# FFN loop: four of eight k-pairs of gate and up as 2x2 block products with seven multiplications

## The chip, the cores and the metric

The kernel runs on one core of one Trainium2 chip. The metric is the time of the core on the device, in microseconds (us); each kernel is run several times and the median counts. Beside the times there is one profiled execution, which gives the time of every instruction on TensorE (PE; its weight load is PEld), VectorE (DVE), ScalarE (ACT), GpSimd (POOL) and in SyncE's queue (SP).

## What is computed

One block of a streaming encoder: retention heads and a state-space group side by side, then a dense SwiGLU FFN. SEQ is 256, D_MODEL 2048, D_FF 5632, all in float32. The change touches the FFN alone:

```python
h = rmsnorm(x, norm_ffn_g[l])
x = x + (jax.nn.silu(h @ w_gate[l]) * (h @ w_up[l])) @ w_down[l]
```

## The kernel before

Every product is made of three matmuls on parts. A float32 matrix is split into a high part (rounded to the matmul's format) and a low part (what is left), and x·w is taken as hi·hi + lo·hi + hi·lo. So each weight is loaded from HBM into `raw`, rounded by ScalarE into `w_hi` (`high`, L492), and VectorE subtracts to get `w_lo` (`low`, L837). `raw`, `w_hi` and `w_lo` have four slots each (RAW = SPL = 4).

The unit of work is a chunk: two k-blocks of 128 rows by 512 columns (512 KB). `column_chunk` (L1510 on, its matmuls L1517) multiplies a chunk with the 256 tokens: 3 parts x 2 k-blocks x 2 halves of 128 tokens = 12 matmuls of 128x128 by 512 columns. The tokens' blocks are the stationary operand, `h2` of `actA` for k-blocks 0 to 7 and of `h2B` for 8 to 15.

D_FF is worked off in 11 groups (FG) of 512 columns. The first group's gate and up chunks, 16 of them (FFN0 to LOOP0), come ahead of the loop. A turn of the loop then has 24 chunks (TURN): 8 of gate and 8 of up of the next group, one k-pair each, and 8 of down of the group before (4 columns of 512, 2 chunks each). There are ten turns, nine in a hardware loop and one written out, and then the tail: 8 down chunks of the last group, and the final norm.

What sets the order: each engine has its program in order, and semaphores count. ScalarE's `high` waits for the data of its chunk (d_raw) and until TensorE has done the chunk four back (pe_done); VectorE's `low` waits for high_done; TensorE's `ready` waits for low_done; SyncE's `load` of the chunk four ahead waits for low_done too. Gate's sum stands in PSUM banks 0 and 1, up's in 2 and 3, down's columns alternate between banks 6, 7 and 4, 5. ScalarE takes silu of gate as soon as gate's 8 chunks are done (`silu`, L767), VectorE multiplies it with up (`ff`, L1152), transposes in blocks (`turn_blocks`, L1179), and SyncE moves the blocks to their places (`move`, L377: two moves behind each of the loads of chunks 5 to 12 of the next turn, the first pair waiting for the transposes). From these ScalarE and VectorE make `ffT_hi` (L772) and `ffT_lo` (L1185) for the down chunks. VectorE adds each down column into x (`down_col`, L1195); TensorE waits for that add (cols_added) before it uses the banks again, two columns later.

## Time and profile before

| | us |
|---|---|
| median of 3 runs | 1118.73 |
| lowest, highest | 1118.14, 1119.39 |
| span of the profiled execution | 1116.8 |
| TensorE busy | 1104.5 |
| VectorE busy | 731.2 |
| ScalarE busy | 533.2 |

The span is what the profiler saw from the first to the last instruction of one execution. Busy time of TensorE is made of matmuls that overlap: a row's own length (389 ns in the list by lines) is longer than the step from one to the next. A row with a count x4 stands for four in a row, with the time from the first's start to the last's end. A step from one operation to the next is read from two starts.

### The profile page before, as it was taken

The numbers are of one execution on the slowest core, as the hardware profiler recorded it, in microseconds if no ns is written. First come the engines' busy times: TensorE is split into PE (matmuls) and PEld (weight loads), VectorE is DVE, ScalarE is ACT, GpSimd is POOL, SyncE is SP. The second block draws the span as 40 slices with busy tenths as digits, with TensorE's granted clock in tenths as the row PEclk, the third lists the DMA queues.
The fourth block names the chain that finished last, engine by engine and source line by source line (L and its number), as shares of the span: only waits on it lengthen the run. The fifth ranks groups of instructions, "written<-read, shape, count | busy, mean of one in ns | idle before, by whom it ended". The sixth has DMA issues, their size and how long they took to land.

```text
span 1116.8 us, 15234 instructions
## 1 busy us (share of the span) xinstructions
PE 1104.5 (99%) x5506; PEld 914.2 (82%) x5506; DVE 731.2 (65%) x811; ACT 533.2 (48%) x640; POOL 106.9 (10%) x162
## 2 busy tenths in 40 slices
PE   9999999999999999999999999999999999999997
PEld 7878778888988888888888888888888888888886
DVE  7999998655865754564655646465564656556477
ACT  7569444345743663434434343443434344443443
POOL 7130233320100500000000000000000000000010
PEclk9999999999999999999999999999999999999999
DMA  9884688854665775867676766757676675757663
GB/s 361 283 227 136 191 225 262 256 167 150 234 207 196 211 225 187 253 196 212 189 212 197 202 198 192 217 189 209 198 204 197 193 214 193 208 194 204 203 209 111
DMA packets 131478, 232.15 MB, mean 208 GB/s; under 512 B 12016, under 2 KB 29808, under 8 KB 130800
## 3 DMA queue, kind: packets, MB, share of 16 engines
q1 hardware_dynamic: 126192, 220.35, 64.0%
q0 software_dynamic: 4832, 10.36, 3.7%
q10 hardware_dynamic: 416, 0.92, 0.2%
q8 instruction: 25, 0.41, 0.1%
q14 instruction: 13, 0.11, 0.0%
HBM read 218.09 MB, written 5.11 MB: 200 GB/s over the span
## 4 chain that ended last, share of the span: by engine, by line
PE 84%; DVE 10%; DMA 3%; issue 2%; ACT 1%; POOL 0%; SPq 0%; POOLq 0%; DVEq 0%; ACTq 0%
PE ps L1517 71%; DVE w_lo L837 4%; PE ps L1542 3%; PE ps L1535 3%; PE ps L1539 3%; DMA raw<-in_w_in 2%; DVE wb L964 1%; DVE wb L962 1%; DVE wb_t L963 1%; PE ps L1817 1%; PE ps L1818 1%; PE ps L1819 1%; PE ps L1650 0%; DVE cl_t L1037 0%; DMA swapped<-state 0%
## 5 line engine op out<-in xcount | busy, mean ns | idle before, releaser
L837 DVE TENSOR_TENSOR w_lo<-raw,w_hi 128x1024 fp32r<-128x1024 f32 x384 | 467.9, 1224 | 355.5 <-ACT w_hi L492 354.6
L492 ACT ACTIVATE w_hi<-raw 128x1024 fp32r<-128x1024 f32 x383 | 406.1, 1061 | 551.5 <-PE ps L1517 428.3
L1517 PE MATMUL ps<-w_hi,actA_hi 128*128 128x512 f32 x416 | 111.4, 390 | 0.0
L1517 PE MATMUL ps<-w_hi,actA_lo 128*128 128x512 f32 x416 | 111.2, 389 | 0.0
L1517 PE MATMUL ps<-w_lo,actA_hi 128*128 128x512 f32 x416 | 111.2, 389 | 0.0
L1517 PE MATMUL ps<-w_hi,h2B_hi 128*128 128x512 f32 x352 | 94.1, 389 | 0.0
L1517 PE MATMUL ps<-w_hi,h2B_lo 128*128 128x512 f32 x352 | 94.1, 389 | 0.0
L1517 PE MATMUL ps<-w_lo,h2B_hi 128*128 128x512 f32 x352 | 94.1, 389 | 0.0
L1517 PEld LDWEIGHTS ps<-w_hi,actA_lo 128*128 128x128 f32 x416 | 78.1, 188 | 16.2
L1517 PEld LDWEIGHTS ps<-w_lo,actA_hi 128*128 128x128 f32 x416 | 78.1, 188 | 16.2
L1517 PEld LDWEIGHTS ps<-w_hi,actA_hi 128*128 128x128 f32 x416 | 77.9, 188 | 16.0
L1517 PE MATMUL ps<-w_hi,ffT_hi 128*128 128x512 f32 x320 | 85.5, 389 | 0.0
L1517 PE MATMUL ps<-w_hi,ffT_lo 128*128 128x512 f32 x320 | 85.5, 389 | 0.0
L1517 PE MATMUL ps<-w_lo,ffT_hi 128*128 128x512 f32 x320 | 85.5, 389 | 0.0
L377 POOL DMA_DIRECT2D ff_moved<-ff_turned x24 | 12.9, 543 | 706.9 <-DVE ff_turned L1179 706.9
L1517 PEld LDWEIGHTS ps<-w_hi,h2B_lo 128*128 128x128 f32 x352 | 66.1, 188 | 13.7
L1517 PEld LDWEIGHTS ps<-w_hi,h2B_hi 128*128 128x128 f32 x352 | 66.1, 188 | 13.7
L1517 PEld LDWEIGHTS ps<-w_lo,h2B_hi 128*128 128x128 f32 x352 | 66.1, 188 | 13.7
L1517 PEld LDWEIGHTS ps<-w_hi,ffT_hi 128*128 128x128 f32 x320 | 60.1, 188 | 12.5
L1517 PEld LDWEIGHTS ps<-w_hi,ffT_lo 128*128 128x128 f32 x320 | 60.1, 188 | 12.5
L1517 PEld LDWEIGHTS ps<-w_lo,ffT_hi 128*128 128x128 f32 x320 | 60.1, 188 | 12.4
L1195 DVE TENSOR_TENSOR x<-ps,x 128x1024 f32<-128x1024 f32 x40 | 48.7, 1218 | 0.0
(279 smaller groups left out, 1261.4 us busy)
## 6 DMA issues: line engine op xcount, KB each, us to landing
raw<-in_w_gate SPq DMA_DIRECT2D x88, 512.0 KB, 4.6
raw<-in_w_up SPq DMA_DIRECT2D x88, 512.0 KB, 4.7
raw<-in_w_down SPq DMA_DIRECT2D x88, 512.0 KB, 4.3
raw<-in_w_in SPq DMA_DIRECT2D x79, 512.0 KB, 5.3
raw<-in_w_out SPq DMA_DIRECT2D x32, 512.0 KB, 4.2
...
raw<-in_ssm_w_glu SPq DMA_DIRECT2D x8, 512.0 KB, 3.4
```

The source lines that it names most:

```text
L377: eng.dma_start(moved[32 * b:32 * b + 32, :, a].rearrange("p t k j -> p t (k j)"), turned[32 * a:32 * a + 32, b].rearrange("p t k j -> p t ...
L492: nc.scalar.activation(w_hi[:, s % SPL], raw[:, s % RAW], ACT.Copy).then_inc(S["high_done"], 1)
L837: tt(w_lo[:, s % SPL], raw[:, s % RAW], w_hi[:, s % SPL].bitcast(F32), ALU.subtract).then_inc(S["low_done"], 1)
L962: tt(o, of_groups(b_re, b, LOC - 1), of_powers(pr, b, 1, LOC - 1), ALU.mult)
L963: link(tt(t, of_groups(b_im, b, LOC - 1), of_powers(pi, b, 1, LOC - 1), ALU.mult))
L964: tt(o, o, t, ALU.add).then_inc(S["wb_ready"], 1)
L1195: tt(cols, ps[:, b0:b0 + 2], cols, ALU.add).then_inc(S["cols_added"], 1)
L1517: ins = mm(ps[:, banks + t], blocks[k][kind == 1][:, tok], w[:, s, at], start=first and kind == 0 and k == 0, stop=last and kind == 2 and ...
L1535: mm(ps[:, banks + t], blocks[k][0][:, tok], w_hi[:, s, at], start=first and k == 0, stop=False)
L1539: mm(ps[:, banks + t], blocks[k][1][:, tok], w_hi[:, s, at], start=False, stop=False)
L1542: ins = mm(ps[:, banks + t], blocks[k][0][:, tok], w_lo[:, s, at], start=False, stop=last and k == 1)
L1817: mm(o, w_hi[:, n % SPL, at], hi, start=first, stop=False)
```

## The change

Gate and up of the same k-pair are now taken together as one pair of chunks, gate's k-pair u in chunk 2u and up's in chunk 2u+1; SyncE loads them in that order. A pair is a product of 2x2 blocks: the tokens' blocks A (2 halves of tokens x 2 k-blocks), the weights' blocks B (2 k-blocks x gate, up). UNITS = "CSCSSCSC" names the pairs 0 to 7: in C (plain) the product takes 8 block products, in S (mixed) 7, by Strassen's scheme in Winograd's form. Each block product is three matmuls, so a plain pair issues 24 and a mixed pair 21.

A mixed pair needs four sums of token blocks (made once, ahead of the loop: `h_column`, `combos`, `combo_high`, `combo_low`), and of weight blocks for every pair anew: VectorE makes four blocks `mix` from raw (`mix_sums`, three operations, two of which wait for the one before), ScalarE rounds them (`mix_high`, 2048 columns), VectorE takes the low part (`mix_low`, 2048 columns). Of the second chunk of the pair only the second half needs a high and a low part of its own (`high_second`, `low_second`, 512 columns). `mix` is one buffer, `mix_hi` and `mix_lo` have two.

The plain pairs add into the same banks as the mixed ones, so they too give sums that are put together at the end: four banks (0 to 3) take plain and mixed products, three (4 to 6) the mixed ones' alone. `first_product`, `first_sums` and `last_sums` put gate and up together in `mix`; silu and `ff` now read `mix`. Banks 4 to 6 are also down's, so pair 1 waits for column 3's add of the turn before and for ff, and down's first column for `first_sums`. VectorE's add of column 3 moves behind the mixed sums of the next turn's pair 1. In `mixed_unit`, TensorE does three products (9 matmuls) on the plain weights, gives both slots back, waits for `mix_low`, and does four (12). g_final shares its place with `mix_lo`; its load moves from ahead of the loop into the tail, behind the last moves.

The core of the diff:

```diff
+UNITS = "CSCSSCSC"
+MIXED = tuple(u for u in range(GRP) if UNITS[u] == "S")
+PLAIN = tuple(u for u in range(GRP) if UNITS[u] == "C")
+NM = len(MIXED)
+B_P2, B_P3, B_P4, B_P5, B_P1, B_P6, B_P7 = range(7)
+COMBO_AT = tuple(FFN0 + 6 + 3 * c for c in range(4))
...
-                        w = A["w_gate"] if c < GRP else A["w_up"]
-                        k = 2 * (c % GRP)
+                        w = A["w_gate"] if c % 2 == 0 else A["w_up"]
+                        k = 2 * (c // 2)
...
+                    sp.wait_ge(S["mix_free"], 1 + NM * (FG - 1))
+                    sp.dma_start(g_final[:], A["g_final"]).then_inc(d_gfin, 16)
...
+            def mix_high(c, turn=None):
+                q = mixed_at(c)
+                act.wait_ge(S["mix_step"], count(turn, 3 * NM, 3 * q + 3))
+                if turn is not None:
+                    act.wait_ge(S["mix_free"], count(turn, NM, q))
+                nc.scalar.activation(mix_hi[:, q % 2], mix[:], ACT.Copy).then_inc(S["mix_high"], 1)
...
+            def mix_sums(c, turn=None):
+                q = mixed_at(c)
+                for s in (LOOP0 + c, LOOP0 + c + 1):
+                    dve.wait_ge(d_raw[s % RAW], count(turn, 16 * TURN // RAW, 16 * (s // RAW + 1)))
+                if c % TURN // 2 != MIXED[0]:
+                    dve.wait_ge(S["mix_low"], count(turn, NM, q))
+                elif turn is not None:
+                    dve.wait_ge(S["ff_ready"], turn + 2)
...
+            def last_sums(j):
+                dve.wait_ge(S["pe_done"], j * TURN + (LOOP0 + 2 * GRP))
+                dve.wait_ge(S["sum_step"], j * 4 + 2)
+                tt(mix[:, 1::2], mix[:, 1:3], ps[:, B_P5].unsqueeze(1).to_broadcast([P, 2, NCOL]), ALU.add
+                   ).then_inc(S["sum_step"], 1)
+                dve.wait_ge(S["sum_step"], j * 4 + 3)
+                tt(mix[:, 0:3], ps[:, B_P2:B_P4 + 1], mix[:, 0:3], ALU.add).then_inc(S["sum_step"], 1)
...
+            def mixed_unit(u, s, q, turn, fresh, done):
+                (a11, a12), (_, a22) = tokens(u, 0), tokens(u, 1)
+                s1, s2, s3, s4 = ([s_mixed[part][MIXED.index(u)][:, k] for part in range(2)] for k in range(4))
+                ends = products([(B_P2, a12, 1), (B_P1, a11, 0), (B_P3, s4, 3)], w_blocks(w_hi, s), w_blocks(w_lo, s),
+                                fresh, done)
+                ends[B_P1].then_inc(S["pe_done"], 1)
+                ends[B_P3].then_inc(S["pe_done"], 1)
+                pe.wait_ge(S["mix_low"], count(turn, NM, q + 1))
+                hi, lo = ([x[:, q % 2, b] for b in range(4)] for x in (mix_hi, mix_lo))
+                ends = products([(B_P5, s1, 0), (B_P6, s2, 2), (B_P7, s3, 1), (B_P4, a22, 3)], hi, lo, fresh, done)
+                ends[B_P4].then_inc(S["mix_free"], 1)
...
+                    if u == MIXED[0]:
                         pe.wait_ge(S["ff_ready"], j + 1)
+                        pe.wait_ge(S["cols_added"], j * 4 + 8)
...
                     if c == 2 * GRP:
                         pe.wait_ge(S["ffT_lo_ready"], j + 1)
+                        pe.wait_ge(S["sum_step"], j * 4 + 2)
```

How it stands in the programs, taken from the last turn of the loop, the one that is written out. TensorE before, gate of k-pairs 1 and 2 (a wait in brackets is a semaphore by name):

```order
L1517 MATMUL ps<-w_hi,actA_hi 128x512 [waits low_done]
L1517 MATMUL ps<-w_hi,actA_hi 128x512 x3
L1517 MATMUL ps<-w_hi,actA_lo 128x512 x4
L1517 MATMUL ps<-w_lo,actA_hi 128x512 x4
L1517 MATMUL ps<-w_hi,actA_hi 128x512 [waits low_done]
L1517 MATMUL ps<-w_hi,actA_hi 128x512 x3
L1517 MATMUL ps<-w_hi,actA_lo 128x512 x4
L1517 MATMUL ps<-w_lo,actA_hi 128x512 x4
```

TensorE after, pair 1, a mixed one, up to the last of its mixed blocks:

```order
L1782 MATMUL ps<-w_hi,actA_hi 128x512 [waits low_done,cols_added,ff_ready]
L1782 MATMUL ps<-w_hi,actA_hi 128x512
L1782 MATMUL ps<-w_hi,sA_hi 128x512
L1782 MATMUL ps<-w_hi,actA_lo 128x512 x2
L1782 MATMUL ps<-w_hi,sA_lo 128x512
L1782 MATMUL ps<-w_lo,actA_hi 128x512 x2
L1782 MATMUL ps<-w_lo,sA_hi 128x512
L1782 MATMUL ps<-mix_hi,sA_hi 128x512 [waits mix_low]
L1782 MATMUL ps<-mix_hi,sA_hi 128x512 x2
L1782 MATMUL ps<-mix_hi,actA_hi 128x512
L1782 MATMUL ps<-mix_hi,sA_lo 128x512 x3
L1782 MATMUL ps<-mix_hi,actA_lo 128x512
```

Between the ninth and the tenth matmul of the pair there is now a wait for `mix_low`, and the wait for low_done at its head counts both chunks. VectorE before, from chunk 4 of the last turn to the product with silu (13 chunks in the first row):

```order
L837 TENSOR_TENSOR w_lo<-raw,w_hi 128x1024 [waits high_done] x13
L1185 TENSOR_TENSOR ffT_lo<-ff_moved,ffT_hi 128x8x4x32 [waits ffT_hi_ready]
L837 TENSOR_TENSOR w_lo<-raw,w_hi 128x1024 [waits high_done] x3
L1152 SCALAR_TENSOR_TENSOR ff_act<-ps,rstd,ff_act 128x512 [waits silu_ready,pe_done]
L1152 SCALAR_TENSOR_TENSOR ff_act<-ps,rstd,ff_act 128x512
```

VectorE after, pairs 3 and 4, both mixed:

```order
L1311 TENSOR_TENSOR mix<-raw 128x1024 [waits mix_low,d_raw3,d_raw2]
L1314 TENSOR_TENSOR mix<-raw,mix 128x512 [waits mix_step]
L1316 TENSOR_TENSOR mix<-raw,mix 128x512 [waits mix_step]
L939 TENSOR_TENSOR w_lo<-raw,w_hi 128x1024 [waits high_done]
L1297 TENSOR_TENSOR w_lo<-raw,w_hi 128x512 [waits high_done]
L1322 TENSOR_TENSOR mix_lo<-mix,mix_hi 128x2048 [waits mix_high]
L1311 TENSOR_TENSOR mix<-raw 128x1024 [waits mix_low,d_raw1,d_raw0]
L1314 TENSOR_TENSOR mix<-raw,mix 128x512 [waits mix_step]
L1316 TENSOR_TENSOR mix<-raw,mix 128x512 [waits mix_step]
L939 TENSOR_TENSOR w_lo<-raw,w_hi 128x1024 [waits high_done]
L1297 TENSOR_TENSOR w_lo<-raw,w_hi 128x512 [waits high_done]
L1322 TENSOR_TENSOR mix_lo<-mix,mix_hi 128x2048 [waits mix_high]
```

Where one low half stood for each chunk, a mixed pair has three sums, a whole and a half low part and a mixed low part, and pair 4's sums stand behind pair 3's mixed low part. VectorE before, around the end of up and the first down column:

```order
L1185 TENSOR_TENSOR ffT_lo<-ff_moved,ffT_hi 128x8x4x32 [waits ffT_hi_ready]
L837 TENSOR_TENSOR w_lo<-raw,w_hi 128x1024 [waits high_done] x3
L1152 SCALAR_TENSOR_TENSOR ff_act<-ps,rstd,ff_act 128x512 [waits silu_ready,pe_done]
L1152 SCALAR_TENSOR_TENSOR ff_act<-ps,rstd,ff_act 128x512
L837 TENSOR_TENSOR w_lo<-raw,w_hi 128x1024 [waits high_done]
L1179 STREAM_TRANSPOSE ff_turned<-ff_act 128x4x4x32 [waits d_moved,ff_ready]
L1179 STREAM_TRANSPOSE ff_turned<-ff_act 128x4x4x32
L837 TENSOR_TENSOR w_lo<-raw,w_hi 128x1024 [waits high_done]
L1195 TENSOR_TENSOR x<-ps,x 128x2x512 [waits cols_added,pe_done]
```

VectorE after, the same place:

```order
L939 TENSOR_TENSOR w_lo<-raw,w_hi 128x1024 [waits high_done]
L1334 TENSOR_TENSOR mix<-ps,mix 128x512 [waits p1_ready]
L1336 TENSOR_TENSOR mix<-ps,mix 128x512 [waits sum_step]
L1342 TENSOR_TENSOR mix<-mix,ps 128x2x512 [waits sum_step,pe_done]
L1345 TENSOR_TENSOR mix<-ps,mix 128x1536 [waits sum_step]
L939 TENSOR_TENSOR w_lo<-raw,w_hi 128x1024 [waits high_done] x2
L1261 SCALAR_TENSOR_TENSOR ff_act<-mix,rstd,ff_act 128x512 [waits silu_ready]
L1261 SCALAR_TENSOR_TENSOR ff_act<-mix,rstd,ff_act 128x512
L939 TENSOR_TENSOR w_lo<-raw,w_hi 128x1024 [waits high_done]
L1371 STREAM_TRANSPOSE ff_turned<-ff_act 128x4x4x32 [waits d_moved,ff_ready]
L1371 STREAM_TRANSPOSE ff_turned<-ff_act 128x4x4x32
L939 TENSOR_TENSOR w_lo<-raw,w_hi 128x1024 [waits high_done]
```

The four sums, the third of which waits for TensorE's last pair, now stand ahead of the low halves of chunks 18 and 19.

## Rows read from the trace of the kernel before

**Rows 1.** Page, part 1; then the chain from 400 us on.

```profile
PE 1104.5 (99%) x5506; PEld 914.2 (82%) x5506; DVE 731.2 (65%) x811; ACT 533.2 (48%) x640; POOL 106.9 (10%) x162
by line: PE ps L1517 97.5%; PE ps L1508 0.5%; PE ps L1507 0.5%; PE ps L1506 0.5%; DVE x_gain L1338 0.1%; POOLq L165 0.1%; ACT y1T L805 0.1%; DVE x L1323 0.1%; DVEq L165 0.1%; POOL ss L1496 0.0%; issue 0.0%; DVEq L1337 0.0%; POOLq L1494 0.0%
```

**Rows 2.** Windows: length, busy us of PE, PEld, DVE, ACT, POOL, granted clock, DMA.

```profile
500.04:565.32 65.28, 65.28 (x290) 54.07 (x288) 37.63 (x33) 27.57 (x27) 0.00 (x0) 1.00 0.68 201
1110.00:1116.80 6.80, 0.00 (x0) 0.00 (x0) 2.50 (x7) 1.44 (x3) 0.92 (x2) 0.81 0.65 250
```

**Rows 3.** Timeline, one chunk: start, us, engine, operation, count, [idle before, releaser].

```profile
714.92 1.07 PE L1517 MATMUL ps<-w_hi,h2B_hi 128*128 128x512 f32 x4
715.12 1.06 ACT L492 ACTIVATE w_hi<-raw 128x1024 fp32r<-128x1024 f32 x1 [1.66 <-PE ps L1517]
...
716.21 1.23 DVE L837 TENSOR_TENSOR w_lo<-raw,w_hi 128x1024 fp32r<-128x1024 f32 x1 [1.49 <-ACT w_hi L492]
...
717.64 1.07 PE L1517 MATMUL ps<-w_hi,actA_hi 128*128 128x512 f32 x4
```

**Rows 4.** By form, TensorE's weight load and VectorE: count, busy us, mean ns.

```profile
L1517 PEld LDWEIGHTS ps<-w_hi,actA_lo 128*128 128x128 f32 x416 | 78.1, 188 | 16.2
L1052 DVE TENSOR_TENSOR qr<-qs,rope 128x512 f32<-128x512 f32 x8 | 5.2, 687 | 5.2 <-PE ps L1641 5.2
```

**Rows 5.** Timeline of VectorE: steps from one operation to the next.

```profile
173.23 1.29 DVE L1052 TENSOR_TENSOR qr<-qs,rope 128x512 f32<-128x512 f32 x2
...
186.53 1.35 DVE L1037 TENSOR_TENSOR cl_t<-c,pi 128x1152 f32<-128x1152 f32 x1
187.92 1.36 DVE L1038 TENSOR_TENSOR cl<-cl,cl_t 128x1152 f32<-128x1152 f32 x1
...
741.83 1.40 DVE L1152 SCALAR_TENSOR_TENSOR ff_act<-ps,rstd,ff_act 128x512 f32<-128x512 f32 x2
...
746.13 1.23 DVE L837 TENSOR_TENSOR w_lo<-raw,w_hi 128x1024 fp32r<-128x1024 f32 x1 [0.28 <-ACT w_hi L492]
747.27 1.22 DVE L1195 TENSOR_TENSOR x<-ps,x 128x1024 f32<-128x1024 f32 x1
```

**Rows 6.** Instructions by form, ScalarE.

```profile
L492 ACT ACTIVATE w_hi<-raw 128x1024 fp32r<-128x1024 f32 x383 | 406.1, 1061 | 551.5 <-PE ps L1517 428.3 <-DMA raw<-in_w_in 56.0 <-PE ps L1542 42.1
L549 ACT ACTIVATE ps<-x_tok 128x2048 f32<-128x2048 f32 x2 | 3.7, 1861 | 0.0
L489 ACT ACTIVATE w_hi<-raw 128x512 fp32r<-128x512 f32 x1 | 0.6, 630 | 0.2 <-DMA raw<-in_w_in 0.2
```

**Rows 7.** DMA issues at 744.8, 761.1, 443.5, 451.2 us; g_final; last: to landing.

```profile
raw<-in_w_gate SPq DMA_DIRECT2D x1, 512.0 KB, 4.5
raw<-in_w_gate SPq DMA_DIRECT2D x1, 512.0 KB, 4.9
raw<-in_w_gate SPq DMA_DIRECT2D x1, 512.0 KB, 5.3
raw<-in_w_up SPq DMA_DIRECT2D x1, 512.0 KB, 6.0
g_final<-in_g_final SPq DMA_DIRECT2D x1, 1024.0 KB, 8.0
```

**Rows 8.** Timelines, the loop's first turn: TensorE's start, SyncE's queue.

```profile
434.76 1.07 PE L1517 MATMUL ps<-w_hi,actA_hi 128*128 128x512 f32 x4
...
440.02 1.27 SPq L377 DMA_DIRECT2D ff_moved<-ff_turned  x2
441.54 0.38 SPq L391 DMA_DIRECT2D raw<-in_w_gate  x1
```

**Rows 9.** Timelines, last down part, tail: TensorE and SyncE's queue.

```profile
1065.80 1.07 PE L1517 MATMUL ps<-w_hi,ffT_hi 128*128 128x512 f32 x4
...
1077.46 13.06 SPq L391 DMA_DIRECT2D raw<-in_w_down  x7
...
1090.28 1.07 PE L1517 MATMUL ps<-w_hi,ffE_hi 128*128 128x512 f32 x4
```

More of the change, by code:

```diff
@@ L328, in h2, with h2_column, count, mixed_at @@
             return (h2B_hi, h2B_lo)[part][:, kb - 8, :]
+        def h2_column(c, part):
+            if c < 2:
+                return (actA_hi, actA_lo)[part][:, 4 * c:4 * c + 4]
+            return (h2B_hi, h2B_lo)[part][:, 4 * c - 8:4 * c - 4]
+        def count(turn, each, n):
+            return n if turn is None else turn * each + n
+        def mixed_at(c):
+            return NM * (c // TURN) + MIXED.index(c % TURN // 2)
+        def mixed_pair(c):
+            return c % TURN < 2 * GRP and c % TURN // 2 in MIXED
+        def column_combos(c):
+            one = 2 * c if 2 * c in MIXED else 2 * c + 1
+            return MIXED.index(one), PLAIN.index(4 * c + 1 - one), one - 2 * c
         def act_block(kb, part):
@@ L690, in side @@
                     x2_square(c)
+                for c in range(4):
+                    if n == COMBO_AT[c] + 2:
+                        combo_high(c)
             def y1T_out(r):
@@ L1145, in out_col_ssm, with ff_first, ff @@
                 last.then_inc(S["cols_added"], 1)
-            def ff(count, chunks):
-                dve.wait_ge(S["pe_done"], chunks)
+            def ff_first():
+                dve.wait_ge(S["pe_done"], LOOP0)
+                dve.wait_ge(S["silu_ready"], 2)
+                for t in range(TOK):
+                    last = stt(ff_act[:, t], ps[:, 4 + t], rstd[:, R_FFN, t:t + 1], ff_act[:, t], ALU.mult, ALU.mult)
+                last.then_inc(S["ff_ready"], 1)
+            def ff(count):
@@ L1277, in _, with down_add @@
                     side(n)
+            for c in range(0, SPL, 2):
+                mixed = mixed_pair(c)
+                if mixed:
+                    mix_sums(c)
+                whole_low(c)
+                side(LOOP0 + c)
+                if mixed:
+                    low_second(c + 1)
+                    mix_low(c)
+                else:
+                    whole_low(c + 1)
+                side(LOOP0 + c + 1)
+            def down_add(j, col):
+                down_col(j * TURN + (LOOP0 + 2 * GRP + 2 * col + 2), j * 4 + (col + 5), col)
             def turn(j, last=False):
                 for c in range(SPL, TURN + SPL):
-                    low(None, turn=j, at=LOOP0 + c)
+                    pair = c < 2 * GRP or c >= TURN and not last
+                    mixed = pair and mixed_pair(c)
+                    if mixed and c % 2 == 0:
+                        mix_sums(c, j)
+                        if c == TURN + 2:
+                            down_add(j, 3)
+                    if mixed and c % 2:
+                        low_second(c, j)
+                        mix_low(c - 1, j)
+                    else:
+                        whole_low(c, j)
                     if c == GRP + SPL + 4:
                         ffT_low(j + 1)
+                    if c == 2 * GRP + 1:
+                        first_sums(j)
+                        last_sums(j)
                     if c == 2 * GRP + 3:
-                        ff(j + 2, j * TURN + (LOOP0 + 2 * GRP))
+                        ff(j + 2)
                     if last and c == 2 * GRP + 4:
@@ L1508, in three, with column_chunk @@
                 return mm(o, x_lo, h, start=False, stop=last)
-            def column_chunk(n, s, blocks, banks, first, last):
+            def column_chunk(n, s, blocks, banks, first, last, frees=None):
                 parts = [(k, t, slice(NCOL * k, NCOL * (k + 1)), slice(P * t, P * (t + 1))) for k in range(2) for t in range(TOK)]
```

213 lines of the change are left out of this document (178 added, 35 removed).

## The prediction

> **What bounds the kernel now.** I read the page first: TensorE is busy 99% of the span and the chain that ended last is almost wholly its matmuls [rows 1]. The windows view then shows that this holds in the loop itself: one turn of the FFN loop takes 65.28 us, TensorE is busy in all of it at a granted clock of 1.00, while VectorE is busy for 38 us and ScalarE for 27.5 us [rows 2]. The timeline of one chunk gives the beat: a chunk of 12 matmuls every 2.72 us, so 0.2267 us each, and 24 chunks in a turn [rows 3]. In the same rows ScalarE rounds a chunk 0.2 us after TensorE has left its slot, VectorE starts its half 1.10 us after that, and both then wait for the next slot. So a turn costs 288 matmuls, and everything else hides. A change that takes matmuls away is worth their beat only as long as the two other engines still hide.
>
> **What goes.** Four of the eight pairs of k-blocks issue 21 matmuls and not 24. That is 12 of 288 in a turn: 12 x 0.2267 = 2.72 us, and 27.2 us over the ten turns. A turn of TensorE alone would be 276 x 0.2267 = 62.56 us. The beat is taken from the row; nothing in it depends on which tile is loaded. The Trainium skill (TensorE: Matmul & The Clock Gate, "Wait — 56ns, not 53.3ns?") has a 512-column matmul at 215.7 ns behind another. The row says 226.7 ns, and the row decides; by the page the gain would be 2.59 us per turn.
>
> **What comes, in engine time.** VectorE's price depends on width only, and neither on SBUF nor PSUM as its source [rows 4, 5]: a 1024-wide operation lets the next one start after 1.14 us; two 512-wide ones together take 1.29 us where one takes 0.687, so a step of 0.60; the rate between them is 1.05 ns per element, which makes 2.22 us for 2048 and 1.68 us for 1536. No row has a tensor_tensor of 2048; the rate is what I have for it. Of width 1152, an operation that waits for the one just before it starts 1.39 us after it, where the rate gives 1.14 + 128 x 1.05 ns = 1.27: 0.11 us more. A mixed pair then takes VectorE 1.25 + 0.71 + 0.60 (the sums, two of them waiting) + 1.14 + 0.60 (the low halves) + 2.22 (the low half of the four mixed blocks) = 6.52 us where it took 2.28. Four of them add 17.0 us. Putting the products together adds 0.71 + 0.60 + 1.25 + 1.68 = 4.2 us. Before, a turn held 24 low halves and 4 column adds (28 x 1.14), the product with silu (1.34), the two transposes (1.27) and the low half of ffT (1.14): 35.7 us. Now it is 56.9 us of 62.6. ScalarE gets 4 x (1.86 + 0.63 - 1.06) + 0.67 = 6.4 us more [rows 6], 34 us in all. So no engine but TensorE is full, but VectorE is at 91%, and in a mixed pair it needs 6.52 us where TensorE needs 21 x 0.2267 = 4.76. What decides is the order within the turn.
>
> **The walk through a steady turn.** T is the time at which TensorE starts pair 0. VectorE gets there with the mixed sums of pair 1, done at T+0.7; column 3's add waited for the last down matmuls and ends at T+1.8; the low halves of chunks 2 and 3 end at T+3.0 and T+3.6. Only then do the slots of raw that pair 3 needs come free. SyncE issues the load of chunk 6 at T+3.1 (0.39 us), then two moves (1.25 us), then chunk 7's at T+4.7. A load lands after 4.5 us when it is alone, after 4.9 with moves beside it, and the second of two in a row after 5.3 [rows 7]. I take 5.3, since this is that case: chunk 7 lands at T+10.0. Before, a slot was refilled in 4.5 us and its chunk came round after 4 x 2.72 = 10.9, so there were 6 us to spare; now the data are wanted at T+8.1, when VectorE is through with pair 2. From there: sums to T+12.6, ScalarE's rounding of 2048 columns to T+14.5, low half to T+16.8. Pair 3 starts at T+15.6 and needs the mixed blocks after 9 matmuls, T+17.7: in time. Pair 4 follows at once as a mixed one: its sums can't start before T+16.8 (one buffer for the sums), end at T+19.3, the low halves of chunks 8 and 9 at T+21.2, its mixed low half at T+23.6. TensorE wants pair 4 at T+20.4 and the mixed blocks 2.0 us later: it waits 0.8, then 0.1, and each wait costs about 0.25 us more, because the weight load (188 ns in [rows 4]) and the start no longer overlap. That is 1.4 us. Pair 6 has the same chain through its loads (issued at T+20.6 and T+22.2, landed T+27.5, mixed low half at T+34.3 against T+34.1): 0.55 us.
>
> The other place is the end of the pairs. VectorE is held at the last sums until pair 7 has ended; call that E. Behind them are queued the low halves of chunks 18 and 19, the product with silu, chunk 20, the transposes, chunk 21 and then the add of column 0, for whose banks column 2 waits: 0.2 + 2.93 + 2.28 + 1.34 + 1.14 + 1.27 + 1.14 + 1.22 = 11.5 us after E, where TensorE comes after 4 chunks, 10.9. With the restart that is 0.9 us. The new wait of column 0 for the first sums costs nothing: pair 7 (5.44 us) hides ScalarE's copy and two 512-wide adds (0.67 + 1.31). Sum: 62.56 + 1.4 + 0.55 + 0.9 = **65.4 us** per turn against 65.28: the 2.72 us go back almost whole.
>
> **Once per run.** In the first turn VectorE arrives late. Before the loop it gets 4 x 3.55 us for the token sums (1.25 + 1.36 + 0.94 each, by widths 1024, 512, 256 and 128), which fill the 1.49 us that it waited per chunk. It reaches the mixed sums of pair 1 only 0.7 us before the loop starts, and then does sums, low halves, the last token sum, mixed low half and the product ff in one piece of 8.8 us; pair 1 waits for ff and is wanted after 5.44: 3.0 us with the restart. The transposes end at 9.4 us after the start of the loop; only then does SyncE issue the moves and behind them the loads of pair 3, as it did before [rows 8]. They land at 17.6 us, the low halves are there at 22.0, pair 3 is wanted at 18.6: 3.7 us. Pair 4 and its mixed blocks follow late by 2.0, pair 6 and column 2 as always, 1.4. So the first turn is 62.56 + 10.1 = 72.7 us. The old first turn had the same late loads, and the four slots hid them. In the tail, the transposes come 2.6 us later and g_final (1 MB, 8.0 us, until now ahead of the loop) lies ahead of the load of chunk 25. That load is issued at 14.8 us after E and not 11.7, lands behind 1 MB more (2 x 1.85 us, two chunks' share by 0.68 of 2.72) at 22.9, and its low half is done at 25.3; TensorE wants it at 24.5 plus the 0.9 from above [rows 7, 9]. I take 0.5 us.
>
> **Sum.** 1116.8 (profiled span) + 9 x 0.1 + 7.4 + 0.5 = 1125.6 us; the waits are sums of small pieces and all on one side, so I round up to 1126.5. The median of the runs is 1.9 us above the span (1118.73): **1128.5 us**, 0.9% slower.
>
> **Bounds.** The turn's waits have unseen parts: the landing of a second load (4.9 to 6.0 in [rows 7], it counts in full in the waits at pair 4 and at pair 6), the restart (0 to 0.25, four times), VectorE's dependent waits (0.11, perhaps 0.05 to 0.2, some eight on the chain). All kind: 1.2 us of waits, 63.8 us per turn, 15 us in all off the forecast. All unkind: 67 us, 16 us on.
>
> **Rivals.** *The matmuls' time is kept.* VectorE has 5.7 us of idle per turn, and if loads land as when alone and restarts are hidden, the walk leaves under 1 us of waits: 63.3 us per turn, 20 us gained, less 7 at the start: 1105 us (1099 to 1113). For it: TensorE never waits now, and half the loads have no move beside them. Against: the chain from T to pair 4 has no slack to begin with. *VectorE's chain becomes the beat.* If the second load takes 6.0 us and each hand-over 0.1 more, pair 4 waits 2.5 us and pair 6 over 1: 66.8 us per turn, 1142 us. It decides from the point where chunk 7 lands later than T+10. *The clock.* The granted clock is 1.00 in all the loop; where TensorE stood idle at the end it is 0.81 [rows 2]. Waits of 3.0 and 3.7 us in the first turn are the longest. If the clock fell to its lower level (1.2 GHz) after one, each 12 matmuls until it rose would cost 2.72 us more, 3 to 5 us once, 1132 us. The Trainium skill has this rule (the same page, "HAM oscillation — how this bites in real kernels"). *That it doesn't do what it says:* the order of instructions has 12 matmuls fewer in each turn, so no.
>
> **Chances.** Forecast (64.9 to 65.9 per turn) 0.42; time kept 0.14; between these two 0.16, of which half ends below 1116.5; VectorE's beat 0.23; clock 0.05. What a measurement can tell from no change is about 0.2%, 2.2 us. So faster 0.22, the same 0.08, slower 0.70. The range leaves out the best case and the worst: 1110 to 1144.
>
> **What would show it.** Right: TensorE's busy share of a middle turn at 96%, turns of 65 to 66 us, its waits at the low halves of pair 4 and at column 2; VectorE about 57 us busy in a turn; first turn near 73 us; loads of chunks 6 and 7 on the path, by a wait of the mixed sums for raw. Wrong: middle turns near 63 us; a 2048-wide operation far from 2.3 us; waits of TensorE at other places; a beat other than 0.2267 us with three or four banks in turn.

## The result, and the profile after

The changed kernel takes **1136.40 us** (median of 4 runs, 1135.68 to 1137.92) against 1118.43 for the kernel before in the same comparison (1117.97 to 1119.39): a ratio of 1.016, 95% interval 1.015 to 1.018. It is slower by 18.0 us, forecast was 9.8. The profiled execution has a span of 1134.4 us against 1116.8.

From the page of the kernel after: busy times (they answer to [rows 1]), and the shares of each engine in the chain that ended last, over the whole span. The third line is the same chain in the kernel before:

```profile
PE 1094.7 (96%) x5386; PEld 891.4 (79%) x5386; DVE 939.1 (83%) x1043; ACT 596.2 (53%) x698; POOL 106.8 (9%) x162
PE 38%; DVE 33%; DMA 11%; issue 8%; ACT 5%; SPq 3%; DVEq 1%; POOL 0%; POOLq 0%; ACTq 0%
PE 84%; DVE 10%; DMA 3%; issue 2%; ACT 1%; POOL 0%; SPq 0%; POOLq 0%; DVEq 0%; ACTq 0%
```

There are 120 matmuls fewer, as intended, and the chain is no longer mostly TensorE: VectorE has a third of it where it had a tenth, and DMA with SyncE's queue 14% where it had 3%. ("issue" is time in which an engine waited for nothing that the profile shows.) The windows view of the kernel after (columns as in [rows 2]) shows the first turn, a middle turn and the tail:

```profile
434.64:507.62 72.98, 66.43 (x277) 53.30 (x276) 60.28 (x60) 33.29 (x32) 0.00 (x0) 0.95 0.60 186
...
573.62:639.58 65.96, 63.79 (x277) 51.49 (x276) 57.16 (x54) 33.49 (x32) 0.00 (x0) 1.00 0.64 199
...
1103.38:1134.40 31.02, 23.84 (x108) 19.85 (x108) 20.79 (x28) 11.93 (x24) 2.61 (x9) 0.89 0.33 121
```

With the starts of the turns from the timeline, the 17.6 us of span add up: the loop starts 0.1 earlier (434.64 against 434.76); the first turn takes 72.98 us, 7.7 more; the next eight run from 507.62 to 1035.96, 66.04 each, 6.1 more together; the last turn 0.1 more; then a wait of 2.1 ahead of the tail, and a tail of 31.02 against 29.24, 1.8 more.

**A middle turn.** It starts at T = 573.62. SyncE's queue, then VectorE, then TensorE, from the timeline (start, us, engine, line, operation; in brackets idle time before, and what ended it):

```profile
576.87 0.38 SPq L428 DMA_DIRECT2D raw<-in_w_gate  x1
577.30 1.24 SPq L414 DMA_DIRECT2D ff_moved<-ff_turned  x2
578.72 0.45 SPq L428 DMA_DIRECT2D raw<-in_w_up  x1
```

```profile
576.61 0.68 DVE L1297 TENSOR_TENSOR w_lo<-raw,w_hi 128x512 fp32r<-128x512 f32 x1
577.21 2.28 DVE L1322 TENSOR_TENSOR mix_lo<-mix,mix_hi 128x2048 fp32r<-128x2048 f32 x1
579.41 2.35 DVE L939 TENSOR_TENSOR w_lo<-raw,w_hi 128x1024 fp32r<-128x1024 f32 x2
584.07 1.22 DVE L1311 TENSOR_TENSOR mix<-raw 128x1024 f32<-128x1024 f32 x1 [2.30 <-DMA raw<-in_w_up]
...
588.81 2.29 DVE L1322 TENSOR_TENSOR mix_lo<-mix,mix_hi 128x2048 fp32r<-128x2048 f32 x1 [0.34 <-ACT mix_hi L544]
591.24 1.23 DVE L1311 TENSOR_TENSOR mix<-raw 128x1024 f32<-128x1024 f32 x1
...
594.97 0.68 DVE L1297 TENSOR_TENSOR w_lo<-raw,w_hi 128x512 fp32r<-128x512 f32 x1
```

```profile
595.71 0.74 PE L1782 MATMUL ps<-w_hi,h2B_hi 128*128 128x512 f32 x2 [1.51 <-DVE w_lo L1297]
596.28 0.39 PE L1782 MATMUL ps<-w_hi,sB_hi 128*128 128x512 f32 x1
...
598.32 0.96 PE L1782 MATMUL ps<-mix_hi,sB_hi 128*128 128x512 f32 x3 [0.25 <-DVE mix_lo L1322]
599.12 0.40 PE L1782 MATMUL ps<-mix_hi,h2B_hi 128*128 128x512 f32 x1
```

The chain of the prediction is there link by link: the half low of chunk 3, two moves between the loads of chunks 6 and 7 in SyncE's queue, the load of chunk 7 issued at T+5.1 and taken up by VectorE at T+10.4, VectorE idle for 2.30 us ahead of pair 3's sums, one buffer that holds pair 4's sums back to 591.24, and TensorE waiting 1.51 us for pair 4's half low and 0.25 for its mixed blocks. Column 2 waits 0.41 more (at 628.55) for column 0's add.

**The first turn.** SyncE's queue and TensorE:

```profile
443.67 1.27 SPq L414 DMA_DIRECT2D ff_moved<-ff_turned  x2
445.19 0.38 SPq L428 DMA_DIRECT2D raw<-in_w_gate  x1
...
447.04 0.45 SPq L428 DMA_DIRECT2D raw<-in_w_up  x1
```

```profile
442.54 0.72 PE L1782 MATMUL ps<-w_hi,actA_hi 128*128 128x512 f32 x2 [2.30 <-DVE ff_act L1254]
...
456.70 1.22 PE L1782 MATMUL ps<-w_hi,actA_hi 128*128 128x512 f32 x2 [3.67 <-DVE w_lo L1297]
457.72 0.63 PE L1782 MATMUL ps<-w_hi,sA_hi 128*128 128x512 f32 x1
...
461.99 0.39 PE L1782 MATMUL ps<-mix_hi,actA_hi 128*128 128x512 f32 x1
```

Pair 1 waits for ff_act and pair 3 for the loads that stood behind the moves. After the second wait the matmuls step by 0.43 us and not by 0.2267: the twelve from 456.70 to 461.99 take 5.29 us instead of 2.72, 2.6 us lost to a clock at its lower level (1.2 of 2.4 GHz; granted over the turn 0.95).

**The tail.** SyncE, ScalarE, VectorE, TensorE:

```profile
1092.93 0.58 SPq L505 DMA_DIRECT2D g_final<-in_g_final  x1
1093.56 12.43 SPq L428 DMA_DIRECT2D raw<-in_w_down  x7
```

```profile
1099.88 1.06 ACT L529 ACTIVATE w_hi<-raw 128x1024 fp32r<-128x1024 f32 x1 [3.93 <-DMA raw<-in_w_down]
```

```profile
1100.97 1.23 DVE L939 TENSOR_TENSOR w_lo<-raw,w_hi 128x1024 fp32r<-128x1024 f32 x1 [3.76 <-ACT w_hi L529]
1102.11 1.22 DVE L1387 TENSOR_TENSOR x<-ps,x 128x1024 f32<-128x1024 f32 x1
```

```profile
1103.38 1.84 PE L1746 MATMUL ps<-w_hi,ffE_hi 128*128 128x512 f32 x4 [2.06 <-DVE x L1387]
1105.02 1.91 PE L1746 MATMUL ps<-w_hi,ffE_lo 128*128 128x512 f32 x4
1106.73 1.27 PE L1746 MATMUL ps<-w_lo,ffE_hi 128*128 128x512 f32 x4
1107.84 1.09 PE L1746 MATMUL ps<-w_hi,ffE_hi 128*128 128x512 f32 x4
```

Chunk 25 lands at 1099.9, behind g_final, and its low half is in time for chunk 25 itself. But column 2's add stands behind it in VectorE's order, and chunk 24 needs that column's banks: 2.06 us, and then twelve matmuls in 4.46 us and not 2.72.

### The profile page after: what moved, and what is told of

It reads as the page before. It is cut to its first block, busy times and chain, and to the rows that moved or that the text cites. A ratio compares the mean times of both kernels' runs of the same rounds, so it can differ in the third digit from the quotient of the medians.

```text
span 1134.4 us, 15538 instructions
## 1 busy us (share of the span) xinstructions
PE 1094.7 (96%) x5386; PEld 891.4 (79%) x5386; DVE 939.1 (83%) x1043; ACT 596.2 (53%) x698; POOL 106.8 (9%) x162
## 4 chain that ended last, share of the span: by engine, by line
PE 38%; DVE 33%; DMA 11%; issue 8%; ACT 5%; SPq 3%; DVEq 1%; POOL 0%; POOLq 0%; ACTq 0%
PE ps L1782 13%; PE ps L1746 12%; DVE w_lo L939 8%; DMA raw<-in_w_up 8%; DVE mix_lo L1322 4%; DVE mix L1311 4%; ACT mix_hi L544 3%; DVE x L1387 3%; PE ps L1773 3%; PE ps L1766 3%; PE ps L1770 3%; DMA raw<-in_w_in 2%; DVE mix L1314 2%; SPq L414 2%; DVE mix L1316 1%
## 5 line engine op out<-in xcount | busy, mean ns | idle before, releaser
L529 ACT ACTIVATE w_hi<-raw 128x1024 fp32r<-128x1024 f32 x343 | 360.5, 1058 | 353.8 <-PE ps L1746 137.4
L939 DVE TENSOR_TENSOR w_lo<-raw,w_hi 128x1024 fp32r<-128x1024 f32 x344 | 411.9, 1218 | 95.9 <-ACT w_hi L529 95.2
L544 ACT ACTIVATE mix_hi<-mix 128x2048 fp32r<-128x2048 f32 x40 | 76.7, 1918 | 81.1 <-DVE mix L1316 81.0
L1322 DVE TENSOR_TENSOR mix_lo<-mix,mix_hi 128x2048 fp32r<-128x2048 f32 x40 | 91.6, 2290 | 9.6 <-ACT mix_hi L544 9.6
L1311 DVE TENSOR_TENSOR mix<-raw 128x1024 f32<-128x1024 f32 x40 | 48.9, 1223 | 39.5 <-DMA raw<-in_w_up 23.9
L1782 PE MATMUL ps<-w_hi,h2B_hi 128*128 128x512 f32 x160 | 53.8, 397 | 11.9 <-DVE w_lo L1297 11.9
L1782 PE MATMUL ps<-w_hi,actA_lo 128*128 128x512 f32 x160 | 53.0, 392 | 0.0
L1782 PE MATMUL ps<-w_lo,actA_hi 128*128 128x512 f32 x160 | 53.0, 392 | 0.0
L1782 PE MATMUL ps<-w_hi,h2B_lo 128*128 128x512 f32 x160 | 52.9, 391 | 0.0
L1782 PE MATMUL ps<-w_lo,h2B_hi 128*128 128x512 f32 x160 | 52.8, 391 | 0.0
```

What stands on the lines that cost most here:

```text
L529: nc.scalar.activation(w_hi[:, s % SPL], raw[:, s % RAW], ACT.Copy).then_inc(S["high_done"], 1)
L544: nc.scalar.activation(mix_hi[:, q % 2], mix[:], ACT.Copy).then_inc(S["mix_high"], 1)
L939: tt(w_lo[:, s % SPL], raw[:, s % RAW], w_hi[:, s % SPL].bitcast(F32), ALU.subtract).then_inc(S["low_done"], 1)
L1311: tt(mix[:, 0:2], b12.unsqueeze(1).to_broadcast([P, 2, NCOL]), raw_blocks[:, first:first + 4:3], ALU.subtract).then_inc(S["mix_step"], 1)
L1322: tt(mix_lo[:, q % 2], mix[:], mix_hi[:, q % 2].bitcast(F32), ALU.subtract).then_inc(S["mix_low"], 1)
L1782: ends[bank] = mm(ps[:, bank], x[kind == 1], w[b], start=kind == 0 and bank in fresh, stop=kind == 2 and bank in done)
```

## The experiments

My theory: the saved 2.72 us a turn are lost in waits, each of which comes from an order in one queue (two moves between two loads; an add behind a low half; ff_first behind pair 1's mixed low; g_final ahead of chunk 25). The main rival: VectorE has 57 of 66 us to work, and the turn is set by that sum, so that a wait taken away in one place comes back in another. Eleven kernels ran. Each is compared with runs of the kernel before on the same chip, whose medians were 1117.7 to 1118.0; beside the changed kernel it was 1118.4. So a difference between a variant and the changed kernel ("less" below) carries up to 0.7 us of such an offset, and the ratios are the safer figures.

### One order at a time

**g_final's load later.** SyncE issues it behind chunk 27's load, and VectorE's wait for it stands ahead of its first use.

```diff
+                if c == 3:
                     sp.wait_ge(S["mix_free"], 1 + NM * (FG - 1))
                     sp.dma_start(g_final[:], A["g_final"]).then_inc(d_gfin, 16)
...
-            dve.wait_ge(d_gfin, 16)
             low(TAIL0 + 4)
...
+            dve.wait_ge(d_gfin, 16)
             gain_col(0)
```

> Only the tail changes: the load of g_final is issued after the loads of chunks 24 to 27 instead of ahead of chunk 25's, and VectorE waits for it right ahead of its first use. Theory (the tail's wait comes from chunk 25's load, issued 0.63 us late and landing 6.3 us later behind g_final's 1 MB; column 2's add is queued behind its low half): the low half of chunk 25 ends near 1100.0 instead of 1102.1, the 2.06 us wait ahead of chunk 24 falls to 0.1 to 0.5, and the matmuls behind it keep the full clock (about 2.1 us): 1132.3 us, 4 less than the changed kernel. Rival (the tail is longer because VectorE's work there comes later anyway): 1136, unchanged, and the wait only changes its place.

Measured 1132.49 us (1131.34 to 1133.72), ratio 1.0124 (1.0107 to 1.0141): 3.9 less than the changed kernel. VectorE's add and TensorE's chunk 24 in its timeline:

```profile
1100.90 1.22 DVE L1388 TENSOR_TENSOR x<-ps,x 128x1024 f32<-128x1024 f32 x1
```

```profile
1102.26 1.11 PE L1747 MATMUL ps<-w_hi,ffE_hi 128*128 128x512 f32 x4
1103.21 1.07 PE L1747 MATMUL ps<-w_hi,ffE_lo 128*128 128x512 f32 x4
```

No wait is left ahead of the tail, and the twelve matmuls behind it keep the full beat. The tail's part is shown.

**The moves not between two loads.** First behind chunks 5, 7, 9 and 11, four at a time:

```diff
-                    if 5 <= c < 13:
+                    if c in range(5, 13, 2):
                         if c == 5:
                             sp.wait_ge(S["turned"], j + (COLS_MOVED + 1))
-                        move(sp, PAIRS[2 * (c - 5):2 * (c - 4)], ff_turned, ff_moved, d_moved)
+                        move(sp, PAIRS[2 * (c - 5):2 * (c - 3)], ff_turned, ff_moved, d_moved)
```

> SyncE issues four moves behind each of chunks 5, 7, 9 and 11 instead of two behind each of 5 to 12, so that no move stands between the two loads of a pair. Theory (the wait at pair 4 is the end of a chain that begins with the late load of chunk 7): that load is issued at T+3.8 instead of T+5.1, the sums of pair 3 start at T+9.1 instead of T+10.45, the wait at pair 4 falls from 1.5 us to 0.2 to 0.9: 0.6 to 1.2 us less in each of nine turns, and the first turn 1.2 longer, since four moves now stand ahead of load 6: 1136.4 - 4 to 10 = 1129. Rival (VectorE's 57 us of work in a turn are the limit, wherever they wait): the same 66.0 us a turn, 1136 to 1137.

Measured 1121.57 us (1119.04 to 1122.90), ratio 1.0029 (1.0019 to 1.0038): 14.8 less, more than the 4 to 10 that I gave, and far from the rival's nothing. Its middle turns take 64.37 us where the changed kernel's take 66.04. SyncE and VectorE in its turn from 571.92:

```profile
575.17 0.38 SPq L428 DMA_DIRECT2D raw<-in_w_gate  x1
575.73 0.38 SPq L428 DMA_DIRECT2D raw<-in_w_up  x1
```

```profile
581.02 1.23 DVE L1311 TENSOR_TENSOR mix<-raw 128x1024 f32<-128x1024 f32 x1 [0.96 <-DMA raw<-in_w_up]
```

Chunk 7's load is issued at T+3.8 and pair 3's sums start at T+9.1, both as expected. The profile then names a wait of TensorE for pair 4's half low in two of the eight turns, 0.5 us in all, where it was 11.0 us in eight turns. The first turn is unchanged at 73 us.

Then the same behind chunks 7, 9, 11 and 13:

```diff
-                    if c in range(5, 13, 2):
+                    if c in range(7, 15, 2):
-                        if c == 5:
+                        if c == 7:
                             sp.wait_ge(S["turned"], j + (COLS_MOVED + 1))
-                        move(sp, PAIRS[2 * (c - 5):2 * (c - 3)], ff_turned, ff_moved, d_moved)
+                        move(sp, PAIRS[2 * (c - 7):2 * (c - 5)], ff_turned, ff_moved, d_moved)
```

> As the one before, with the four moves behind chunks 7, 9, 11 and 13. Theory: middle turns as there (0.6 to 1.2 us less); in the first turn the loads of chunks 6 and 7, which now wait behind the wait for the first transposes, are issued at about 437.2 and 438.8 instead of 445.2 and 447.0, so that the 3.67 us wait at pair 3 and the halved clock behind it (2.4 us) go and some 1 us appears instead: first turn 67 to 68 instead of 73.0, in all 1136.4 - 11 (8 to 16) = 1125. If the moves now come too late for the turned activations, a wait appears at column 0 (TensorE's first down matmul). Rival (VectorE's throughput): first turn shorter, middle turns still 66.0: 1131.

Measured 1114.89 us (1112.68 to 1118.03), ratio 0.9970 (0.9956 to 0.9983): 21.5 less than the changed kernel (I gave 8 to 16), and now 0.3% faster than the kernel before. SyncE's queue in the first turn, and the windows of first and second turn:

```profile
437.65 0.37 SPq L428 DMA_DIRECT2D raw<-in_w_gate  x1
439.05 0.37 SPq L428 DMA_DIRECT2D raw<-in_w_up  x1
443.92 2.54 SPq L414 DMA_DIRECT2D ff_moved<-ff_turned  x4
```

```profile
434.64:502.65 68.01, 65.29 (x278) 52.99 (x277) 60.49 (x60) 33.41 (x32) 0.00 (x0) 0.97 0.64 201
502.65:566.88 64.23, 63.56 (x277) 51.59 (x276) 57.17 (x54) 33.66 (x32) 0.00 (x0) 1.00 0.62 204
```

The loads no longer stand behind the wait for the transposes; pair 3 does not wait at all, and the turned activations are in time. The wait of 2.30 us at pair 1 is still there, and this time the clock falls behind it (granted 0.97 over the turn). VectorE works as long as before (57.17 us) in a turn that is 1.8 us shorter. That alone contradicts the rival.

**The column's add ahead of the low half** of the same step (chunks 21, 23, 25, 27):

```diff
+                    if c >= 2 * GRP + 5 and c % 2:
+                        col = (c - 2 * GRP - 5) // 2
+                        if col < 3 or last or not mixed_pair(TURN + 2):
+                            down_add(j, col)
                     if mixed and c % 2:
                         low_second(c, j)
                         mix_low(c - 1, j)
...
-                    if c >= 2 * GRP + 5 and c % 2:
-                        col = (c - 2 * GRP - 5) // 2
-                        if col < 3 or last or not mixed_pair(TURN + 2):
-                            down_add(j, col)
```

> VectorE adds a down column's sums ahead of the low half that it now stands behind (chunks 21, 23, 25 and 27), and nothing else is changed. Theory (column 2 waits for column 0's add only because of VectorE's order): 0.41 us of wait and 0.25 of restart go in each of nine turns, and so do the tail's 2.06 us wait, its restart and its slow matmuls (2.1), since column 2's add no longer stands behind the late chunk 25: 1136.4 - 5.9 - 4.4 = 1126 (1121 to 1130). Rival: the low half of chunk 21 is 1.1 us later and TensorE waits for that, or the turn is set by VectorE's sum of work: within 1 us of 1136 in the loop, 4 less in the tail, 1132.

Measured 1120.83 us (1120.25 to 1123.33), ratio 1.0028 (1.0018 to 1.0037): 15.6 less, just below the range that I gave. One of its middle turns:

```profile
635.53:700.40 64.87, 63.67 (x277) 51.58 (x276) 57.42 (x54) 33.55 (x32) 0.00 (x0) 1.00 0.65 201
```

The wait ahead of the tail is gone in its profile, and so are all waits at column 2. Its middle turns take 64.81 us, 1.23 less and not 0.66: the waits at pair 4 shrank with them, from 1.38 us on average to 0.94. The add, the low halves and the next turn's sums form one queue on VectorE, and I had looked at one link of it: VectorE now starts the mixed sums of pair 1 at T-2.5 instead of T-1.9 (means of eight turns), the load of chunk 7 goes out at T+4.7 instead of T+5.1, and pair 4's low halves are done 0.5 us sooner. It is the same chain, begun earlier; the table at the end of the experiments has it.

### All orders together

**ff_first earlier**, on top of the moves behind chunk 7:

```diff
-                if n == LOOP0 + 3:
+                if n == LOOP0 + 2:
                     ff_first()
+                if n == LOOP0 + 3:
                     turn_blocks(1, None)
```

> The kernel with the moves behind chunks 7, 9, 11 and 13 (1114.9 us), and VectorE takes the first turn's activations out of their banks (ff_first) ahead of the half low and the mixed low of pair 1 instead of behind them. Theory (the 2.30 us wait at pair 1 in the first turn is only VectorE's order): it falls to 0.3 to 0.6, 1.7 to 2 us less, of which a later pair may take back up to 1.5 where the loads of chunks 6 and 7 are not in time: 1113.5 (1112.8 to 1114.9). Rival (the loads of pair 2 and 3 set the first turn): a wait of the same size appears at pair 2 or 3, and it stays at 1114.9.

Measured 1112.20 us (1111.49 to 1113.46), ratio 0.9946 (0.9930 to 0.9963): 2.7 less. The 2.30 us wait at pair 1 is gone; pair 2 now waits 0.40 (at 444.71) and pair 4 1.00. The median is 0.6 below what I gave as the lowest. I had left the clock out: in the profile before this edit it falls behind the wait at pair 1 and once more in the tail, here in neither place.

**All four edits.**

> All four edits together: moves behind chunks 7, 9, 11 and 13, down columns' sums ahead of the low halves, ff_first earlier, g_final's load behind chunk 27's. Theory (each takes away a wait of its own chain): from 1114.9 the column 2 waits go (0.66 us in each of nine turns, 5.9), the tail's wait and slow matmuls (4.3), and 1.4 of the first turn: 1103 us (1099 to 1107), turns of 63.1 to 63.8 us where TensorE's own work is 62.56. Rival (VectorE's sum of work is the next bound): it would wait for nothing in a turn and TensorE's waits would gather anew: turns stay at 64.4, 1109.

Measured **1099.38 us** (1098.51 to 1100.76), ratio **0.9825** (0.9809 to 0.9842). Its page and its windows, first turn, a middle one, the last, the tail:

```profile
PE 1083.7 (99%) x5386; PEld 890.7 (81%) x5386; DVE 941.0 (86%) x1043; ACT 596.9 (54%) x698; POOL 106.6 (10%) x162
```

```profile
434.25:499.99 65.74, 64.04 (x278) 51.44 (x277) 60.78 (x61) 33.65 (x32) 0.00 (x0) 1.00 0.63 205
...
563.19:626.18 62.99, 62.99 (x277) 51.75 (x276) 57.50 (x54) 33.67 (x32) 0.00 (x0) 1.00 0.65 208
...
1006.09:1069.35 63.26, 63.12 (x277) 51.73 (x276) 56.27 (x52) 34.02 (x33) 4.31 (x8) 1.00 0.64 207
1069.35:1098.60 29.25, 22.07 (x109) 18.60 (x107) 20.84 (x28) 12.76 (x25) 2.63 (x9) 0.93 0.45 172
```

The middle turns take 63.26 us on average. VectorE does 57.5 us in 63, and TensorE waits for it 1.2 us in all of eight turns. So the two large gains per turn, 1.59 us (moves behind chunk 7, 64.45) and 1.23 us (adds), add up (2.82 one by one, 2.78 together), and the rival's "it comes back elsewhere" is not seen. Against the changed kernel the span is 35.8 us shorter: 0.4 ahead of the loop, 7.2 in the first turn, 22.2 in eight turns, 4.2 in the last turn with its wait, 1.8 in the tail.

**The mixed pairs elsewhere.** With all four edits, the mixed pairs at 1, 3, 5, 6, and at pair 3 the whole low half of chunk 6 ahead of the sums:

```diff
-UNITS = "CSCSSCSC"
+UNITS = "CSCSCSSC"
...
+                    if low_first and c % 2 == 0:
+                        s = LOOP0 + c
+                        dve.wait_ge(S["high_done"], j * TURN + (s + 1))
+                        tt(w_lo[:, s % SPL], raw[:, s % RAW], w_hi[:, s % SPL].bitcast(F32), ALU.subtract)
                     if mixed and c % 2 == 0:
                         mix_sums(c, j)
```

> As the one before, with the mixed pairs at 1, 3, 5 and 6 instead of 1, 3, 4 and 6, so that a plain pair follows pair 3, and at pair 3 VectorE makes the whole low half of chunk 6 ahead of the mixed sums, while it waits for chunk 7's load. Theory (the two mixed pairs in a row behind the late load are what is left of the chain): turns of 62.6 to 63.3 us, 0.5 to 1 less in each of ten, 1098 (1093 to 1103). Rival (the wait belongs to any two mixed pairs in a row, since one buffer of sums serves all): it moves to pair 6, and the time stays at that of the one before.

Measured 1101.01 us (1100.83 to 1101.40), ratio 0.9843 (0.9826 to 0.9859): no gain, though the time lies in the range that I gave. The rival was right. The wait is at the second of two mixed pairs in a row, wherever they stand: now 0.19 us at pair 6 in each of eight turns, which take 63.28 us.

> The kernel with all four edits (1099.4 us, turns of 63.0 to 63.9), with the mixed pairs at 1, 2, 4 and 6 instead of 1, 3, 4 and 6: the two in a row now come ahead of the chunks that are loaded beside the moves. Theory (what is left of a middle turn's wait, 0.2 to 0.6 us at pair 4, comes from two mixed pairs in a row right behind the late load): turns of 62.8 to 63.2, 1097 (1095 to 1100), and the first turn may lose up to 1. Rival (column 3's add and the mixed sums of pair 1 at the start of a turn leave VectorE no time for pair 2): waits of 1 us and more at pair 2, 1105 to 1110.

```diff
-UNITS = "CSCSSCSC"
+UNITS = "CSSCSCSC"
```

Measured 1103.41 us (1102.21 to 1104.76), ratio 0.9876 (0.9859 to 0.9892), slower than at 1, 3, 4 and 6, and between what the two theories gave. In its profile the middle turns take 63.4 us, 0.1 more than in the others: pair 2, again the second of two mixed pairs in a row, waits 0.16 to 0.28 us in each for its mixed blocks. It waits 2.45 us once, in the first turn. Placement is worth little once the queues are in order.

**The same orders in the kernel before.**

> The kernel before, with no Strassen pairs, and two of the edits: moves behind chunks 7, 9, 11 and 13, and the down columns' sums ahead of the low halves. Theory (these orders matter only where VectorE has little time left, and TensorE waits nowhere in the loop of the kernel before): 1118, unchanged (1117 to 1119). Rival (the edits help whatever the kernel, by calmer transfers or a steadier clock): 3 to 15 us less.

Measured 1118.20 us (1117.45 to 1119.02), ratio 0.9997 (0.9988 to 1.0007). These two orders cost nothing there and bring nothing (the other two were not tried there): with 38 us of VectorE work in a turn and four slots of slack every link had time. It was the change that made them matter.

### One sum more, in two places

Both kernels are the changed kernel with one added sum of 128x1024 per turn on VectorE, whose result isn't used.

```diff
                     if mixed and c % 2 == 0:
+                        if c == 6:
+                            extra()
                         mix_sums(c, j)
```

> The changed kernel (1136.4 us), and VectorE does one more sum of 128x1024 a turn, whose result nobody reads, right ahead of the mixed sums of pair 3, where it waits 2.30 us for chunk 7's load. Theory (the turn is set by the chain from that load): the extra 1.14 us lie inside the wait: 1136.4, unchanged within 1.5. Rival (VectorE's sum of work sets the turn): 1.14 us more in each of ten turns, 1148.

```diff
                         mix_sums(c, j)
+                        if c == 8:
+                            extra()
```

> The changed kernel, with the same extra sum behind the mixed sums of pair 4 and ahead of that pair's low halves, for which TensorE waits 1.5 us. Theory (chain): every microsecond put there comes out at TensorE: 1.14 us more in each of nine or ten turns, 1147 (1145 to 1149), and the wait at pair 4 is 2.6 us; the difference to the kernel with the sum in the gap is the proof, since VectorE's work is the same. Rival (sum of work): the same time as that kernel, 1148 both, or 1136 both if VectorE has slack wherever the sum stands.

In the gap: 1134.68 us (1133.15 to 1136.12), ratio 1.0152 (1.0135 to 1.0168). Behind the load: 1152.09 us (1148.34 to 1156.76), ratio 1.0296 (1.0276 to 1.0317). The kernel with the sum in the gap, VectorE and a window:

```profile
580.45 1.22 DVE L1492 TENSOR_TENSOR h_sum<-x 128x1024 f32<-128x1024 f32 x1
582.76 1.23 DVE L1311 TENSOR_TENSOR mix<-raw 128x1024 f32<-128x1024 f32 x1 [1.09 <-DMA raw<-in_w_up]
```

```profile
506.93:572.39 65.46, 63.81 (x277) 51.51 (x276) 58.31 (x55) 33.64 (x32) 0.00 (x0) 1.00 0.64 200
```

The kernel with the sum behind the load, two windows, and TensorE after one of its waits at pair 4:

```profile
576.21:644.11 67.90, 64.16 (x277) 51.36 (x276) 58.22 (x55) 33.52 (x32) 0.00 (x0) 1.00 0.63 194
644.11:713.58 69.47, 66.43 (x278) 53.66 (x276) 58.31 (x55) 33.41 (x32) 0.00 (x0) 0.95 0.60 188
```

```profile
667.55 1.22 PE L1789 MATMUL ps<-w_hi,h2B_hi 128*128 128x512 f32 x2 [2.63 <-DVE w_lo L1297]
668.57 0.63 PE L1789 MATMUL ps<-w_hi,sB_hi 128*128 128x512 f32 x1
```

VectorE is busy for 58.3 us a turn in both. In the gap the idle time only shrinks, and the turn stays (65.72 us on average; the changed kernel has 66.04). Behind the load the turn takes 67.86. The sum of VectorE's work does not set the turn; its place does.

The second result is 5 us above what I gave. The wait at pair 4 grew by 1.08 us, as priced (1.14), but the sum also adds waits at pair 6 (0.24 to 0.44 us in three of the eight turns) and, in four of them, a fallen clock: the four turns without it take 67.45 us on average, the four with it 68.27. The first result is 1.7 us under the changed kernel, but against the kernel before on its own chip it is 17.0 us slower where the changed kernel is 18.0, and the intervals of the two ratios overlap: no difference is shown. In its last turn pair 3 waits 1.08 us, because its load of chunk 7 took 7.2 us to land. VectorE stood idle for 3.13 us ahead of the sums even so, and the added sum is not the cause. The kernel with the sum behind the load has such a landing in its last turn too (6.9 us); why is not shown.

The chain in six of the kernels, means of the eight middle turns of each profile, in us from T. TensorE is through with pair 3 at T+20.6 in each of them:

| kernel | load of chunk 7 issued | landed | pair 4's low halves done | idle ahead of pair 4 | turn |
|---|---|---|---|---|---|
| changed kernel | 5.09 | 10.14 | 21.92 | 1.38 | 66.04 |
| moves behind 5, 7, 9, 11 | 3.80 | 8.74 | 20.51 | 0.09 | 64.37 |
| column's add first | 4.72 | 9.67 | 21.45 | 0.94 | 64.81 |
| all four orders | 3.44 | 8.36 | 20.13 | 0.04 | 63.26 |
| sum in the gap | 5.09 | 9.88 | 21.66 | 1.15 | 65.72 |
| sum behind the load | 5.09 | 10.13 | 23.04 | 2.46 | 67.86 |

## Why the prediction was right, and where it was off

The sign, the mechanism and the range held: 1136.4 in 1110 to 1144, a range 34 us wide. The size was off: 18.0 us slower and not 9.8, and a middle turn at 66.04 us lies just outside the 64.9 to 65.9 to which I had given 0.42. Point by point:

- **What goes** was right: 120 matmuls, at a beat of 0.2267 us with three or four banks in turn (three of them from 445.62 to 446.30). In pairs 4 to 7 some steps are 0.23 to 0.24.
- **What comes** was right to 2%: VectorE 57.16 us against 56.9, the 2048-wide low half 2.20 us to the next operation against 2.22, ScalarE 33.5 against 34.
- **The walk** was right in its links and 0.4 to 0.8 us early at its end. The load of chunk 7 was issued at T+5.1 and not T+4.7, landed 5.2 us later (5.3 said), and pair 4's low halves were done at T+22.0 and not T+21.2. That the first link, the load behind two moves, sets it is shown by moving them: 14.8 and 21.5 us.
- **The mis-sized term** is the middle turn's waits, 3.48 us over TensorE's own 62.56 where I had 2.85. The waits that the profile names are 2.13 of them: in eight turns 11.0 us at pair 4, 2.7 at mixed blocks, 3.3 at column 2. The other 1.35 are 10.8 us in eight turns. 8.7 of these lie at the 27 waits, so a restart is 0.32 us where I had 0.25: 0.17 because idle time counts from the end of the last matmul (0.39 us after its start, where the next one would start after 0.2267), 0.12 in the three steps behind the wait, the first of which is 0.33 to 0.34, and 0.03 in the next ones. The rows above show it: behind the wait two steps take 0.57 us and not 0.45, three take 0.80 and not 0.68. The last 2.1 us, 0.26 a turn, lie away from these waits, and I had them at nothing: half are steps of 0.23 to 0.24, most of them in pair 6, half are ten single longer steps, too short for the profile to name a wait. By place, with restarts: pair 4 costs 2.3 us and not 1.4, pair 6 0.2 and not 0.55, column 2 0.7 and not 0.9. So the sum came as near as it did because errors of both signs stood in it. Over the nine turns all this makes 5.3 us of the 8.8 by which the sum (1125.6) fell short of the span. The 0.9 by which I rounded up had no term behind it.
- **The tail** is the step that failed, 3.8 us where I took 0.5. I compared chunk 25's low half with chunk 25's own time and found it nearly in time, as it was. I did not ask what is queued behind it on VectorE: column 2's add, which chunk 24 needs. The two runs that took away either half of this (g_final's load, the order of add and low half) both remove the wait.
- **The first turn** came out (72.98 for 72.7), but not by its parts. The wait at pair 1 was 2.30 and with its restart 2.6, where I had 3.0; at pair 3 it was 3.67, 4.0 with the restart for 3.7. The 2.0 at pair 4 was 0.17, since TensorE spent 2.6 us more in pair 3 at the lower clock. That the total agreed is luck. The clock rival, with 0.05, had the right mechanism twice: here, where it hid behind another wait, and in the tail, 1.7 us.
- **Rivals.** "VectorE's chain becomes the beat" is the same chain with larger pieces, and the result lies between it and the forecast, in time nearer to the rival (1142 and 1128.5 for 1136.4). Its point of decision, chunk 7 landing later than T+10, was just passed (T+10.1 on average); its pieces did not come: the load took 5.1 us on average and not 6.0, pair 4 waited 1.4 and not 2.5, pair 6 0.1 and not over 1. "The matmuls' time is kept" (1105) is what the kernel with all four orders does, 1099.4; the time was there, and four orders in two queues, SyncE's and VectorE's, stood in its way.
